# Router logits with tokens on rows in a two-layer decoder trunk, and longer PE fillings around the routing

## What is computed

```
logits = jnp.dot(xf.astype(F32), w_router.astype(F32))     # xf (512, 1024), w_router (1024, 8)
top_logit, top_e = lax.top_k(logits, TOP_K)                 # TOP_K = 2
gates = jax.nn.softmax(top_logit, axis=-1)
e_flat = top_e.reshape(-1).astype(jnp.int32)
order = jnp.argsort(e_flat)                                 # tokens sorted by expert
counts = jnp.bincount(e_flat, length=N_EXPERTS)
padded = (counts + ROW_BLOCK - 1) // ROW_BLOCK * ROW_BLOCK  # ROW_BLOCK = 128
...
return (jax.nn.silu(xb @ w1[e]) * (xb @ w3[e])) @ w2[e]     # per block of an expert's tokens
```

## Time and profile before

| | us |
|---|---|
| median of 3 runs | 2054.57 |
| lowest, highest of the 3 | 2053.45, 2057.57 |
| the profiled execution | 2053.44 |
| its span, first to last instruction | 2051.7 |
| mean granted PE clock, share of full | 0.995 |

### The profile page before, as it was taken

How to read it: one execution, slowest core, us unless ns; L and a number is a source line. 1 busy time by engine, 2 the same in 40 slices (tenths; PEclk the granted TensorE clock), 3 DMA queues, 4 the chain that set the end, 5 groups by cost and what they waited for, 6 DMA issues and landing times.

```text
span 2051.7 us, 34464 instructions
## 1 busy us (share of the span) xinstructions
PE 1995.0 (97%) x12302; PEld 1765.2 (86%) x12303; DVE 1567.6 (76%) x1977; ACT 1103.8 (54%) x1273; POOL 115.7 (6%) x104
## 2 busy tenths in 40 slices
PE   7999999999999999899999999999999999999997
PEld 6889887877779788899999988888999888999875
DVE  6866535353557585888888899999888898888997
ACT  6532433232335423555655577777555677555775
POOL 0000000000000000300100010100100101000340
PEclk9999999999999999999999999999999999999999
DMA  5312723232322123877787799999777899877992
GB/s 197 103 62 93 264 85 102 82 102 82 107 78 83 65 70 142 235 264 260 240 276 245 249 343 378 361 382 361 270 264 259 294 388 344 277 247 247 347 410 108
DMA packets 218608, 449.51 MB, mean 219 GB/s; under 512 B 13248, under 2 KB 64464, under 8 KB 218560
## 3 DMA queue, kind: packets, MB, share of 16 engines
q1 hardware_dynamic: 210416, 421.05, 58.7%
q0 software_dynamic: 8144, 27.82, 3.6%
HBM read 431.87 MB, written 16.96 MB: 219 GB/s over the span
## 4 chain that ended last, share of the span: by engine, by line
PE 82%; DVE 11%; issue 3%; ACT 3%; DMA 0%; DVEq 0%; ACTq 0%; SPq 0%; POOLq 0%
PE ps L613 17%; PE ps L615 17%; PE ps L614 17%; PE ps L955 12%; PE ps L972 8%; PE ps L957 5%; PE ps L974 3%; DVE w_lo L1834 2%; DVE w_lo L1831 2%; PE ps L682 1%; ACT w_hi L1240 1%; DVE w_lo L1388 1%; PE ps L637 1%; DVE ex L1413 1%; ACT w_hi L1242 0%
## 5 line engine op out<-in xcount | busy, mean ns | idle before, releaser
L1831 DVE TENSOR_TENSOR w_lo<-raw,w_hi 128x1024 fp32r<-128x1024 f32 x336 | 409.4, 1218 | 78.7 <-ACT w_hi L1240 75.6
L955 PE MATMUL ps<-xt,w_hi 128*128 128x304 f32 x1792 | 457.1, 345 | 2.9 <-DVE xt L1845 2.5
L957 PE MATMUL ps<-xt,w_lo 128*128 128x152 f32 x1792 | 420.0, 234 | 0.0
L1240 ACT ACTIVATE w_hi<-raw 128x1024 fp32r<-128x1024 f32 x340 | 357.6, 1052 | 106.5 <-PE ps L957 56.3
L1834 DVE TENSOR_TENSOR w_lo<-raw,w_hi 128x1024 fp32r<-128x1024 f32 x336 | 408.9, 1217 | 0.0
L1242 ACT ACTIVATE w_hi<-raw 128x1024 fp32r<-128x1024 f32 x340 | 356.6, 1049 | 1.2 <-DMA raw<-in_moe_w_dram 1.2
L957 PEld LDWEIGHTS ps<-xt,w_lo 128*128 128x128 f32 x1792 | 342.9, 191 | 0.1
L955 PEld LDWEIGHTS ps<-xt,w_hi 128*128 128x128 f32 x1792 | 338.8, 189 | 3.5 <-issue 3.4
L613 PE MATMUL ps<-act_hi,w_hi 128*128 128x512 f32 x608 | 242.1, 398 | 5.2 <-DVE act_lo L1432 5.2
L615 PE MATMUL ps<-act_hi,w_lo 128*128 128x512 f32 x608 | 239.9, 395 | 0.0
L614 PE MATMUL ps<-act_lo,w_hi 128*128 128x512 f32 x608 | 239.9, 394 | 0.0
(11 more groups left out here) (361 smaller groups left out, 3230.4 us busy)
## 6 DMA issues: line engine op xcount, KB each, us to landing
raw<-in_moe_w_dram SPq DMA_DIRECT2D x672, 512.0 KB, 5.2
raw<-in_w_in_dram SPq DMA_DIRECT2D x19, 1024.0 KB, 5.1
raw<-in_ffn_w_gate_dram SPq DMA_DIRECT2D x11, 1024.0 KB, 5.3
raw<-in_ffn_w_up_dram SPq DMA_DIRECT2D x11, 1024.0 KB, 5.4
raw<-in_ffn_w_down_dram SPq DMA_DIRECT2D x11, 1024.0 KB, 4.8
raw<-in_w_out_dram SPq DMA_DIRECT2D x8, 1024.0 KB, 4.9
y_rows<-mult POOLq DMA_DIRECT2D x1, 8192.0 KB, 28.6
y_rows<-yacc POOLq DMA_DIRECT2D x7, 512.0 KB, 5.5
```

The source lines that it names most:

```text
L955: pe.matmul(pairs_of(ps[:, bank, 0:2 * NW]), hi_[:, k % 4, f * P:(f + 1) * P], xt[:, k, :, 0:NW], start=k == 0, stop=False)
L957: last = pe.matmul(ps[:, bank, NW:2 * NW], lo_[:, k % 4, f * P:(f + 1) * P], xt[:, k, 0, 0:NW], start=False, stop=k == KT - 1)
L1240: act.activation(slot_hi[p % 6][:, 0:half], raw6(p)[:, 0:half], ACT.Copy).then_inc(w_hi_half, 1)
L1831: dve.tensor_tensor(slot_lo[p % 6][:, 0:half], raw6(p)[:, 0:half], f32(slot_hi[p % 6][:, 0:half]), ALU.subtract)
```

## The change

The logits are formed with tokens on rows. A slice's 128 tokens of `act_hi` or `act_lo` are the weights, and the router's columns move: the high and rest parts stand side by side in one tile `wr_parts`, 16 columns for each `act_hi` slice, and the 8 of the high part for each `act_lo` slice. For 8 slices and 4 groups of 128 tokens these are 64 matmuls, into 64 columns of bank 0. The high-part and rest-part sums stay in separate columns, and DVE adds them in one reduction straight out of PSUM, in place of the copy to `rt`. The copy to `fold`, the four turning products, the filling of 7 and two semaphores go. The other fillings become 28, 24 and 35. SP's fourth piece waits for `logits_done`.

```diff
-        fold = at("fold", [P, CW], F32, yturned0)
-        wr_hi = at("wr_hi", [P, KT, NE], F32R, yturned0 + 4608)
-        wr_lo = at("wr_lo", [P, KT, NE], F32R, yturned0 + 4864)
+        wr_parts = at("wr_parts", [P, KT, 2 * NE], F32R, yturned0 + 4608)
+        wr_hi, wr_lo = wr_parts[:, :, 0:NE], wr_parts[:, :, NE:2 * NE]
...
                     elif first and p_static[0] == 3:
-                        sp.wait_ge(logits_turned, 1)
+                        sp.wait_ge(logits_done, 1)
...
             pe.wait_ge(wr_split, 2)
+            def logits(k, tt, part):
+                a_ = (act_hi, act_lo)[part][:, k, tt * P:(tt + 1) * P]
+                n = 2 * NE * tt
+                if part:
+                    return pe.matmul(ps[:, 0, n:n + NE], a_, wr_parts[:, k, 0:NE], start=False, stop=False)
+                return pe.matmul(ps[:, 0, n:n + 2 * NE], a_, wr_parts[:, k, :], start=k == 0 and tt == 0,
+                                 stop=k == KT - 1 and tt == NT - 1)
+
             for k in range(KT):
+                pe.wait_ge(*((in_hi, 3 * KT + k + 1) if k else (in_lo, 3 * KT + 1)))
+                if k < KT - 1:
+                    for tt in range(NT):
+                        logits(k, tt, 0)
                 pe.wait_ge(in_lo, 3 * KT + k + 1)
-                last = mm3(ps[0:NE, 0, :], wr_hi[:, k, :], wr_lo[:, k, :], act_hi[:, k, :], act_lo[:, k, :],
-                           k == 0, k == KT - 1)
-            last.then_inc(logits_turned, 1)
-            spin(ps[:, 7, 0:P], 7)
-            pe.wait_ge(logits_copied, 1)
+                for tt in range(NT):
+                    logits(k, tt, 1)
             for tt in range(NT):
-                last = pe.matmul(ps[:, 1, tt * NE:(tt + 1) * NE], fold[0:NE, tt * P:(tt + 1) * P],
-                                 idt[0:NE, 0:NE], start=True, stop=True)
+                last = logits(KT - 1, tt, 0)
             last.then_inc(logits_done, 1)
-            spin(ps[:, 7, 0:P], 24)
+            spin(ps[:, 7, 0:P], 28)
             pe.wait_ge(route_ready, 1)
...
-            spin(ps[:, 7, 0:P], 13)
+            spin(ps[:, 7, 0:P], 24)
             pe.wait_ge(pick_ready, 1)
...
-            spin(ps[:, 7, 0:P], 14)
+            spin(ps[:, 7, 0:P], 35)
             turned_next = pe.alloc_register("pe_turned_next")
             pe.wait_ge(items_ready, 1)
...
-            dve.wait_ge(logits_turned, 1)
-            dve.tensor_copy(fold[0:NE, :], ps[0:NE, 0, :]).then_inc(logits_copied, 1)
             dve.wait_ge(logits_done, 1)
...
-            link(dve.tensor_copy(rt[:, LG, :], ps[:, 1, 0:NT * NE]))
+            parts = ps[:, 0, 0:2 * NE * NT].rearrange("p (t a e) -> p t e a", a=2, e=NE)
+            link(dve.tensor_reduce(r3(LG), parts, AX.X, ALU.add))
```

More of the change, by code:

```diff
@@ L320, in build @@
         wr_split = sem("wr_split")
-        logits_turned = sem("logits_turned")
-        logits_copied = sem("logits_copied")
         logits_done = sem("logits_done")
```

## The result

The kernel after takes 2064.11 us (median of 6, 2061.38 to 2067.27) against 2053.23 (2050.91 to 2057.57) for the kernel before on the same chip: ratio 1.0053, 95% interval 1.0043 to 1.0062, so 10.9 us slower. It was timed once more later, as h1: 2066.59 against 2053.66, ratio 1.0058 [1.0038, 1.0078]. The direction was forecast, the size not: 2059.0 was named and 2062.5 was the top of the range.

A forecast was written before the change was run, and what follows sets the result against it. DVE was taken to bound the kernel from 811.10 into the first expert, PE ahead of that. Logits plus 3.8 and fillings plus 0.6 gave 4.4 us: 2057.8 profiled, 2059.0 named with 1.1 for the median; range 2054.0 to 2062.5.

The forecast's parts named there:

- A: Routing, first logit product to last `xt` subtraction: the clock falls in the short products, shifting it 4.4 us later.
- 806.0: Moment in the logits at which PE's clock was expected to fall, with 23 products done and 41 remaining.
- the 4.7 us of the sum: 28 fillings before the ranks: 16 at the low clock, 12 at the full one, 4.7 us against 3.0.
- the late picks: Pick products after the ranks: PE 1.1 us late behind 24 fillings, hidden by 3.0 us of cover.
- the fourth weight piece: SP's weight transfer, issued at 814.7 in place of 809.1: hidden; without its slack it would cost 5.6 us.
- Rival A: Logits: the clock holds at 1.00, 0.4 us saved, 2054.2; chance 12%.
- the bounds: Fall of the clock in the logits: 1.5 us either way, from 804.5 to 807.5.
- rival B: Logits to ranks: the low clock outlasts the ranks, plus 6.9 to 8.4 us, 2061.5 and over; chance 10%.
- the forecast case: Clock falls in the logits and returns in the fillings, costing 3.0 to 6.0 us; chance 75%.
- The saving at full clock: Logits without a fall of the clock: 0.4 us saved in sum.
- That gain is worth nothing: First expert: 35 fillings remove the low clock at 831.40, some 1.6 us of PE work, but PE then waits for DVE.
- costs nothing: First expert: PE's lateness of 0.9, up to 1.9 us, is free because PE waits for DVE later.

The follow-up runs named there:

- e4: Kernel after with the fillings of before (24, 13 and 14), its PE loop 256 instructions behind before's place: 2057.72 us, ratio to before 1.0028.
- h3: h2 with 14 fillings in place of 35 ahead of the first expert: 2064.38 us, ratio to before 1.0042.
- e2: Kernel after with 133 extra PE instructions, putting its expert loop 256 instructions behind before's place: 2063.09 us, ratio to before 1.0052.
- h2: e2 timed again, beside the kernel after on the same chip: 2062.02 us, ratio to before 1.0041.
- f1: e2 with each logit product widened to 128 columns by reading the 16 columns eight times: 2058.11 us, ratio to before 1.0021.
- f3: Kernel before with 35 fillings in place of 14 ahead of the first expert, PE loop padded by 256 instructions: 2058.27 us, ratio 1.0021.
- e1: Kernel before with 123 extra PE instructions that do nothing, ahead of the loop over experts: 2060.79 us, ratio 1.0040.
- f4: e3 with the two idle stretches of the spread (PE's closing products with `chosen`) filled: 2052.90 us, ratio to before 0.9995.
- e3: Kernel before with the fillings of after (28, 24 and 35), PE loop padded by 256 instructions: 2057.85 us, ratio 1.0030.

## Why the prediction missed

**Right.** The mechanism of A and nearly all its terms. In h1 the clock fell at 806.03, and 806.0 was written; that they agree so closely is luck, since h1 came to the logits 1.0 us sooner and the fall is 3.5 us into them and not 2.5. Short products went from 0.111 to 0.213 us apart, the 28 fillings took the 4.7 us of the sum (812.96 to 817.67), and DVE read the ranks 16.4 us behind the first logit product; 17.1 was predicted, 12.7 it was before. From DVE's read of the ranks to the end of `xt` it is 13.74 us in before (816.24 to 829.98), in h1 and in after: the late picks are hidden, as worked out. e4's B, 1202.27, shows the fourth weight piece hidden too. Rival A (the clock holds) is out in all six profiles with the narrow products. The rule of the Trainium skill that the prediction had beside it ("TensorE: Matmul & The Clock Gate", Why this matters for your kernels), which warns of idle gaps alone, doesn't cover h1's windows. The fall's moment has the wide play that the bounds said and more: 0.7, 1.8, 2.3, 3.4, 3.5 and 3.6 us behind the first narrow product in after, h3, e2, e4, h1 and h2. In after's first profile A is 6.9 longer, which is rival B's "plus 6.9" by luck: the clock was back at 820.2, ahead of the ranks, and B had it low beyond them. It is the forecast case with the fall still earlier than its bound (804.5, 1.0 us into the logits, plus 6.0).

**Mis-sized.** The saving at full clock: 0.4 was put down, f1 (the clock held, 128 columns) measures 0.2 in A, its products 0.112 apart in place of 0.108. And A as a whole: 4.4 was put down, h1 has 3.7 and e4 3.2.

**Wrong: "That gain is worth nothing", and the lateness behind it "costs nothing".** The step took PE's work to be all that a low clock in slack changes. It changes the waits too: with the fall at 831 in slack, PE arrives late at DVE's results and waits in two short pieces; without it, it waits in one long piece and the clock falls there (f3, +0.9 in B). With the same filling came the fall in the spread, in f3's profile and, to judge by their times, in its other runs. The lateness itself was in no run without the rest, so it stays untested. Inside after, going back to 14 alone wins nothing (h3), since the 28 and 24 ahead of it change the pattern as well; only with all three fillings back, as in e4, is B before's.

**Missing: the instruction stream.** The sum has terms for what the added instructions do and none for where they put the code behind them. In h1 5.2 us, about half of the whole, came in B, from a pause of 3.55 and a fall of the clock with it; e1 has the same without any of the rest. It could have been asked: the chain of before has 3% of "issue", and its longest branch was 411 ns at that very jump.

**Missing: the spread.** 1200 us behind the change, and not touched by it: +3.5 less 1.3. The prediction took for granted that time lost ahead just shifts what follows. Here the spread lost the clock in every profile with a fall at 863 to 873 or at the long branch, except where its idle stretches were filled (f4). Whether the earlier fall does it, or the shift that comes with it, no run parts.

The sum by h1: -1.0 + 3.7 + 5.2 + 3.5 - 1.3 = 10.1 us, and 2063.47 less 2053.44 is 10.0. What stays open: why the jump is cheap at before's place, by what the fall in the spread hangs on the earlier one, and how much of the difference in medians comes from falls ahead of the logits.

## To carry to other kernels

Products with few moving columns can lose PE's clock even when PE never pauses; before 64 of them replace 24 long ones, count what they cost at 0.213 and not at 0.11 us. When a kernel has a loop or a branch behind the edit, look at the branch rows of both traces first: an edit that adds instructions can cost microseconds by moving a jump, and the old kernel with as many idle instructions tells (e1). And a low clock that lies in slack may be worth keeping: filling the idle time ahead of it moved the fall to where it hurt (f3).

## What the hardware showed that I had not expected

- A branch on PE took 0.41 or 3.4 to 3.7 us at its first jump over the other kind's code, by the place of the code alone; the median of that line's twelve branches is 0.17.
- With PE busy all the time, the clock went with the columns of a product: 64 products of 8 and 16 lost it in all six profiles that have them, of 128 in one of two, of 256 in none of two. Two profiles each are few.
- Changes of the clock keep step with each other and not with the program: in seven profiles the fall in the spread starts 1170.77 us behind the one at 863 to 873 (f3: 864.66 and 2035.43; h3: 873.11 and 2043.88), to 0.01 us, while B differs by 1.7 among them. In the five that kept the clock in the spread, the next fall comes 1211.73 behind the one at 830 to 838, after the last product.
- Idle stretches of 0.60 and 0.65 us, amid products of 24 and 128 rows, are enough to lose 5 us at the end, where a fall at 863 came before (e3 against f4).
